# Interleaving the token-mean products of a Fourier mix with its first output tile, and taking two half tiles before the rest

## The reference, cut to what matters

```
def fourier_mix(a, w_out):
    B, L, D = a.shape
    ag = a.reshape(B, L, FNET_GROUPS, FNET_GROUP_DIM).astype(jnp.float32)
    f = jnp.fft.fft2(ag, axes=(1, 3), norm="ortho").real
    return f.astype(a.dtype).reshape(B, L, D) @ w_out

def first_block(x, c, ...):
    sh1, sc1, gt1, sh2, sc2, gt2 = ada_params(c, w_mod[i], b_mod[i])
    a_lat = modulate(h_lat, g_norm_mix[i], sh1, sc1)
    y_lat = fourier_mix(a_lat, w_fnet_out[j])
    h_lat = h_lat + gt1 * y_lat
    h_lat = h_lat + gt2 * conv_ffn(modulate(h_lat, g_norm_ffn[i], sh2, sc2), ...)
```

## Time and profile before

| what | value |
|---|---|
| median of 3 runs | 1563.52 us (1563.16 to 1564.2) |
| the profiled execution, own time | 1563.37 us |
| its span | 1561.6 us |
| TensorE busy | 1544.6 us, 99% |
| GpSimd busy | 999.9 us, 64% |
| VectorE busy | 748.0 us, 48% |
| ScalarE busy | 310.2 us, 20% |
| share of the chain that ended last | TensorE 96% |

### The profile page before, as it was taken

How to read it: one execution, slowest core, us unless ns; L and a number is a source line. 1 busy time by engine, 2 the same in 40 slices (tenths; PEclk the granted TensorE clock), 3 DMA queues, 4 the chain that set the end, 5 groups by cost and what they waited for, 6 DMA issues and landing times.

```text
span 1561.6 us, 19509 instructions
## 1 busy us (share of the span) xinstructions
PE 1544.6 (99%) x7096; PEld 1287.6 (82%) x7096; DVE 748.0 (48%) x876; ACT 310.2 (20%) x478; POOL 999.9 (64%) x792
## 2 busy tenths in 40 slices
PE   7999999999999999999999999999999999999998
PEld 6998888888887888888888888888888888888887
DVE  7875455560427565244154665456576434443013
ACT  6542111110111001112032122212322111111001
POOL 4736666666666666766555576475567667676664
PEclk9999999999999999999999999999999999999999
DMA  9962333333332333332323232232233333333231
GB/s 371 404 241 81 94 103 98 94 95 94 99 112 86 96 101 100 106 95 81 107 68 95 72 96 86 80 94 81 67 94 95 94 99 100 97 94 94 95 102 61
DMA packets 218119, 172.52 MB, mean 110 GB/s; under 512 B 5216, under 2 KB 191968, under 8 KB 218080
## 3 DMA queue, kind: packets, MB, share of 16 engines
q1 hardware_dynamic: 218080, 171.98, 35.2%
HBM read 169.86 MB, written 2.10 MB: 110 GB/s over the span
## 4 chain that ended last, share of the span: by engine, by line
PE 96%; DVE 1%; DMA 1%; SPq 1%; issue 0%; ACT 0%; DVEq 0%
PE ps L572 32%; PE ps L575 32%; PE ps L576 32%; DMA mod_early<-in_w_mod_t 1%; DVE act_lo L1402 0%; SPq L314 0%; SPq L322 0%; PE ps L655 0%; PE ps L905 0%; DVE gates L1750 0%; DVE mod_early L1313 0%; PE ps L759 0%; DVE res L1522 0%; SPq L334 0%; PE ps L688 0%
## 5 line engine op out<-in xcount | busy, mean ns | idle before, releaser
L550 POOL TENSOR_TENSOR w_lo<-raw,w_hi 128x1024 fp32r<-128x1024 f32 x248 | 623.0, 2512 | 20.7
L572 PE MATMUL ps<-act_hi,w_hi 128*128 128x512 f32 (+1 forms) x1304 | 506.1, 388 | 0.2 <-DVE act_lo L1402 0.2
L576 PE MATMUL ps<-act_lo,w_hi 128*128 128x512 f32 (+1 forms) x1304 | 503.0, 386 | 0.0
L575 PE MATMUL ps<-act_hi,w_lo 128*128 128x512 f32 (+1 forms) x1304 | 503.0, 386 | 0.0
L547 POOL TENSOR_TENSOR w_hi<-raw,zero 128x1 fp32r<-128x1 f32 x248 | 56.2, 226 | 488.5 <-PE ps L572 488.5
L572 PEld LDWEIGHTS ps<-act_hi,w_hi 128*128 128x128 f32 x1304 | 245.7, 188 | 51.5 <-issue 1.7
L575 PEld LDWEIGHTS ps<-act_hi,w_lo 128*128 128x128 f32 x1304 | 245.7, 188 | 49.7 <-issue 1.4
L576 PEld LDWEIGHTS ps<-act_lo,w_hi 128*128 128x128 f32 x1304 | 245.7, 188 | 49.2
L548 POOL TENSOR_SCALAR w_hi<-raw 128x1023 fp32r<-128x1023 f32 x248 | 266.5, 1075 | 0.0
L572 PE MATMUL ps<-wide_hi,w_hi 128*128 128x512 f32 (+2 forms) x624 | 239.9, 384 | 0.4 <-DVE wide_lo L1281 0.4
L576 PE MATMUL ps<-wide_lo,w_hi 128*128 128x512 f32 (+2 forms) x624 | 239.4, 384 | 0.0
(11 more groups left out here) (193 smaller groups left out, 1440.2 us busy)
## 6 DMA issues: line engine op xcount, KB each, us to landing
raw<-in_w_in SPq DMA_DIRECT2D x88, 512.0 KB, 4.0
gates<-in_w_mod_t SPq DMA_DIRECT2D x20, 1024.0 KB, 11.3
raw<-in_w_ffn_up SPq DMA_DIRECT2D x40, 512.0 KB, 3.9
raw<-in_w_ffn_down SPq DMA_DIRECT2D x22, 512.0 KB, 3.7
raw<-in_w_ff_gate SPq DMA_DIRECT2D x22, 512.0 KB, 3.9
raw<-in_w_ff_up SPq DMA_DIRECT2D x22, 512.0 KB, 3.9
raw<-in_w_ff_down SPq DMA_DIRECT2D x22, 512.0 KB, 3.8
raw<-in_w_r_out SPq DMA_DIRECT2D x16, 512.0 KB, 3.5
```

The source lines that it names most:

```text
L550: nc.gpsimd.tensor_tensor(w_lo[:, two, :], raw[:, slot, :], f32(w_hi[:, two, :]), SUB).then_inc(split_done, 1)
L572: ins = mm(o, w, a, start=start, stop=False)
L575: mm(o, wl, a, start=False, stop=False)
L576: return mm(o, w, al, start=False, stop=stop)
```

## The change

Four things change, and no product is added or left out.

1. On TensorE the 16 token-mean products no longer stand in one block. Two of them follow each of the eight products of the second half of mix tile 0. The wait ahead of them is for one Fourier tile more (`3 * (KT - 1)`), because `dc_psum` moves from bank 3 to bank 5.
2. The second half of mix tile 1 comes next, ahead of the wait for column 0. Tile 1 is thus taken in two halves of 256 tokens, where it was one piece of 512.
3. Panel 1 is split earlier: `fnet_hi(1)` on ScalarE ahead of the loop over the Fourier tiles, `fnet_lo(1)` on GpSimd ahead of the eight low parts `act_lo`.
4. SyncE's and VectorE's code stays as it is.

```diff
+DC_BANK = 5
...
-        dc_psum = ps[:, 3, 0:KT]
+        dc_psum = ps[:, DC_BANK, 0:KT]
...
             fnet_lo(0)
+            fnet_lo(1)
...
-            for m in range(1, 6):
+            for m in range(2, 6):
                 fnet_lo(m)
...
-            pe.wait_ge(f_made, 3 * (KT - 2))
-            pe.wait_ge(dc_step, DC_SUMMED)
-            for m in range(KT):
+            def dc_products(m):
+
                 g, e = m // 2, m % 2
                 for k in range(2):
                     c0 = k * 2 * GROUP + e * P
                     ins = mm(dc_psum[:, m:m + 1], raw[:, 2, c0:c0 + P], udc[:, 2 * g + k:2 * g + k + 1], start=k == 0, stop=k == 1)
-            ins.then_inc(dc_step, 1)
+                return ins
...
+            pe.wait_ge(f_made, 3 * (KT - 1))
+            pe.wait_ge(dc_step, DC_SUMMED)
+            t_ = halves[1]
+            pe.wait_ge(fnet_split, 1)
+            for b in range(KT):
+                pe.wait_ge(f_ready, b + 1)
+                product(ps[:, FNET_BANKS[0], t_], *w_block(fnet_weights(0), b), act_hi[:, b, t_], act_lo[:, b, t_], b == 0, b == KT - 1)
+                ins = dc_products(b)
+            ins.then_inc(dc_step, 1)
+            pe.wait_ge(fnet_split, 2)
+            tile(ps[:, FNET_BANKS[1], t_], None, fnet_weights(1), act_hi[:, :, t_], act_lo[:, :, t_])
+            pe.wait_ge(dc_step, DC_READY)
+
             for n, (m, t_) in enumerate(FNET_TILES):
...
-                if n == 0:
-                    t_ = halves[1]
-                    tile(ps[:, FNET_BANKS[n], t_], None, fnet_weights(m), act_hi[:, :, t_], act_lo[:, :, t_], (f_ready, 0))
-                    pe.wait_ge(dc_step, DC_READY)
+                if n < 2:
                     t_ = halves[0]
...
             shift_sum(2)
+            fnet_hi(1)
...
             f_hi(KT - 1)
-            fnet_hi(1)
             act.wait_ge(dc_step, DC_DONE)
```

## The result

| | before | changed |
|---|---|---|
| median | 1563.99 us (1563.16 to 1565.1, 14 runs) | 1567.39 us (1566.72 to 1568.91, 14 runs) |
| ratio | | 1.0022, 95% interval 1.0015 to 1.0029 |
| profiled execution, span | 1561.6 us | 1565.5 us |

The change costs 3.4 us, more than the 3.1 us (0.2%) that I had called the bound of what can be told, though the interval reaches down to 0.15%. The forecast was 1564.2, the range ended at 1565.7.

A forecast was written before the change was run, and what follows sets the result against it. TensorE has 96% of the chain, but the DMA queue sets the time at `half_sums(0)`, swallowing TensorE's 1.11 us gain. 1563.37 + 0.7 of hole = 1564.1, stated as 1564.2 for the median; 8-in-10 range 1562.9 to 1565.7.

The forecast's parts named there:

- TensorE's own sum: TensorE from token-mean products to start of tile 2: 16.30 us before, 15.19 after, a gain of 1.11 us.
- Panel 1's split: Earlier split on ScalarE and GpSimd fits their idle gaps; first low part 0.5 us late, cost 0 on the path.
- DC_DONE 3.0 us later: Signal that the last token-mean product is done, awaited by ScalarE, VectorE and SyncE: at 55.12 instead of 52.10.
- VectorE's cover: VectorE's existing 3.2 us of DMA waits between 60 and 75 us absorb its 3.0 us delay at column 0.
- A hole of 0.7 us: DMA engines idle 0.7 us before panel 3, issued at 55.3; all later landings and the squares slip by 0.7.
- The clock: Rival, 12%: TensorE's idling at `half_sums(0)` drops its clock, costing 0.7 + 1.6 us; 1565.8.
- a wait of 2.0 us: TensorE reaches `half_sums(0)` at 91.95 and waits for squares ready at 94.0, where it waited 0.25 us.
- The rival on the other side: Slower, 8%: clock falls early in the interleaved stretch, panel 3 is issued later, hole of 2.2 to 2.7 us; 1566.0.
- The "Nothing" rival: Rival, 20%: transfers in flight at 55.3 hide panel 3's start, TensorE's gain still lost at `half_sums(0)`; 1563.5, +-0.2.
- The rival of a gain: Rival, 12%: squares tied to TensorE's own pieces, not a DMA landing, so `half_sums` comes earlier; -1.1 us, 1562.4.

The follow-up runs named there:

- e6: Changed kernel with the token-mean products in one block again, ahead of the second half of tile 0; 1565.32 us, ratio 1.0008 to before.
- e9: Changed kernel, SyncE issuing part 4's first chunk ahead of the wait for the token-mean products, panels 3 and 5 in old order; 1563.69 us.
- e2: Changed kernel, VectorE working on two more tiles of part 2 before it waits for column 0; 1567.07 us, ratio 1.0022 to before.
- e7: Kernel before, SyncE's issue of panel 3 held until panel 2's low part is done, 4.9 us later; 1568.78 us, ratio 1.0031.
- e3: Kernel before, SyncE's issue of panel 3 held until panel 1's low part is done, 2.5 us later; 1565.20 us, ratio 1.0009.
- e10: e9 with first-half sums moved behind the fourth product of piece 10 and second-half sums one step later; 1562.94 us, ratio 0.9993 to before.
- e11: e10 run once more, nothing further changed; 1562.90 us, ratio 0.9994 to the kernel before.
- e1: Changed kernel, SyncE issuing panel 5 and part 4's first chunk ahead of panel 3; 1567.30 us, ratio 1.0014 to before.
- e4: Changed kernel with 24 surplus products of 256 columns on TensorE ahead of `half_sums(0)`, result unread; 1565.69 us, ratio 1.0013 to before.

## Why the prediction was wrong

- **TensorE's own sum: right in kind, a little large.** Tile 2 starts at 64.30, 64.05 without this execution's 0.25; forecast 63.9. The gain is 0.86 us instead of 1.11. The clock held in this stretch, as said. Most of the missing 0.25 is a later start, 49.14 where 48.75 and the offset give 49.00, and the eight interleaved groups, 6.45 us (49.14 to 55.59) instead of 6.37.
- **Panel 1's split: right.** The next copy on ScalarE came at 39.97, and TensorE saw no new wait. e6 and e9 have it and lose no 3 us by it.
- **DC_DONE 3.0 us later: nearly right.** Column 0 on ScalarE is at 55.76, forecast 55.3, and 0.25 of the difference is this execution's: 3.2 us later.
- **VectorE's cover: right.** It was held 3.1 us and then waited for the DMA again: its tile of 72.23 stands at 74.65, released by a landing. e2 takes away 2.4 us of the hold, and the squares stay late.
- **"A hole of 0.7 us": the step that failed.** It measured 1.9 us in the share of the DMA engines and 2.1 in the squares. The landing of panel 3 itself was what I said: issued at 55.8, landed 3.3 us later, 0.97 later than before and 0.72 without the offset. But I took the lateness of this one landing for the idle time of the engines, and as the sum's only term it put the squares at +0.7.

Three things were missing in that step. Quarter microseconds of the changed kernel show the first two:

```profile
54.00:54.25 0.25, 0.25 (x4) 0.25 (x4) 0.00 (x0) 0.00 (x0) 0.00 (x0) 1.00 1.11 426
54.25:54.50 0.25, 0.25 (x5) 0.25 (x4) 0.00 (x0) 0.00 (x0) 0.00 (x0) 1.00 0.77 287
...
54.75:55.00 0.25, 0.25 (x4) 0.25 (x4) 0.00 (x0) 0.00 (x0) 0.00 (x0) 1.00 0.48 189
...
55.50:55.75 0.25, 0.25 (x4) 0.25 (x4) 0.00 (x0) 0.00 (x0) 0.00 (x0) 1.00 0.25 98
...
56.25:56.50 0.25, 0.25 (x4) 0.25 (x3) 0.25 (x1) 0.25 (x1) 0.00 (x0) 1.00 0.00 0
56.50:56.75 0.25, 0.25 (x5) 0.25 (x4) 0.25 (x1) 0.25 (x1) 0.00 (x0) 1.00 0.00 0
...
57.50:57.75 0.25, 0.25 (x5) 0.25 (x4) 0.25 (x1) 0.00 (x0) 0.25 (x1) 1.00 1.00 410
```

First, the 16 DMA engines run dry one after the other. The trace records 16 steps of the semaphore for each transfer, and the landing is the last of them. Panel 4's came from 54.74 to 56.85, so most engines had nothing to do long before the landing (issued at 39.35, 17.5 us to landing). Second, panel 3, issued at 55.80, has its first packet at 56.77, 0.97 us later (0.96 in e7), and the share is back at 1.00 from 57.50. The delay at the other end is shorter: panel 4's last packet ended at 56.36, 0.49 us before its landing. Third, the landing of panel 3 hid the hole. In the kernel before its 16 steps were spread from 55.59 to 58.13, in the changed kernel from 58.64 to 59.11: on average they came 2.3 us later, the last only 0.98. Behind the hole all engines started together, so the slowest one had caught up with the others.

The landings behind it were 1.1 us late (without the offset of 0.25) up to the second chunk, and 2.1 from panel 6 on. At the second of these steps the profile shows one packet of another DMA queue, which starts at 66.06 and takes 0.96 us. From the DMA view of 66 to 68 us (queue and kind, packets, MB, share of 16 engines):

```profile
q8 instruction: 1, 0.02, 3.0%
```

Panel 6's last step came 1.08 us behind the last but one, where the chunk ahead of it had 0.15, and the distance stayed. The same shows in e3 and e7 behind their packet at 70.9 and 70.7; in the kernel before, with its steps still spread over some 2.4 us, the packet at 70.7 moved the last step hardly at all. That this packet is what put one engine back is inferred from time and size, not tested. By this reading the squares would have been only some 1.1 us late without it (an estimate), and that 1.9 us of idle share went with 2.1 us of late squares is in part chance.

How far the queue covers a late issue can be read off the profiled executions. Panel 3's issue was at 55.09 in e3, 55.46 in e2, 55.80 in the changed kernel and 57.38 in e7, and the squares were 1.69, 1.96, 2.37 and 3.90 us late. Each issue less its lateness gives 53.4 to 53.5; in e9 the chunk's issue, at 53.12, was ahead of that, and there was no hole. It fits the share, which falls from 54.25 on, less the 0.97 us from issue to first packet. The kernel before issued at 52.3 and had 1.1 us to spare; the change moved the issue by 3.5.

The Trainium skill (DMA: Bandwidth & Descriptors, "Anatomy of one DMA") says that most of a DMA's fixed cost of some 2.0 us lies behind the last byte, in the confirmation of the write; it says so of DMAs that GpSimd issues, and here SyncE issues them. The trace doesn't agree with this split: 0.97 us lie ahead of the first packet and 0.49 behind the last. Its sum of an estimated 3.2 us for the landing, used in the prediction, was near the measured 3.3.

- **The clock: a rival at 12%, and it came.** I priced it rightly (1.6; measured 1.5) and its sum, 1565.8, lacked only the larger hole: 1565.8 + 1.4 = 1567.2. It was probably the failed step that brought it on: I forecast a wait of 2.0 us, and it was 3.04; no run had one of 2.0. Waits of 1.0 (e9) and 1.6 us (e3) left the clock alone in the profiled executions, 3.04, 3.6 and 3.9 lost it, and one of 3.0 (e2) kept it.
- **The rival on the other side** had the wrong place (the clock inside the interleaved stretch). Its remark that the hole decides, and not VectorE, held.

The "Nothing" rival falls with e3: what is in flight hides only the first 1.1 us of a later issue. The rival of a gain falls too, but e10 and e11 show what it would have needed.

Open: the single runs of the kernel before lie in two groups, around 1563.2 and around 1564.8. A clock that falls behind the block of token-mean products in some executions and not in others would do it, but no profile without that fall was taken.

## What to carry to other kernels

Where an order is changed on one engine, look for the DMA issue that waits for the moved work: in a stretch where the DMA engines are full, the time to protect is when the first engines run dry, which the DMA share shows and a landing doesn't (here the share fell from 54.25 on and the landing came at 56.85). The issue has to come about another microsecond ahead of that (0.97 us from issue to first packet here). Each microsecond by which it missed that time was a microsecond for what hangs on later landings (e3, e7). Put a transfer that is free to go ahead of the one that waits, but no more than fills the hole, since what waits behind may itself release a later issue (e1). A gain on the bounding engine counts only up to its next wait in program order; move the wait into the work (e10). An idle stretch can cost the clock on top: here those of 3.04, 3.6 and 3.9 us did, those of 1.0 and 1.6 us and one of 3.0 us didn't.

## What the runs showed of the hardware

- Surplus matmuls in an idle stretch made the program 1.4 to 1.7 us faster (e4); the granted clock behind it stayed at 1.00 instead of 0.50.
- Single-column float32 products, 32 instructions in a row, were shown as 3.50 of 3.50 us busy and were followed by half the clock. With three 256-column products between every four of them the clock held at 1.00 in the executions that I profiled.
- A 512 KB DMA issued into a nearly empty queue landed after 3.3 us; in the full queue of the kernel before it took 5.8.
- The 16 steps of one transfer's semaphore came 2.1 us apart from first to last (changed kernel, panel 4), and 0.5 us apart behind a stretch in which all engines had been idle (panel 3).
- From an issue on SyncE to its first packet with all DMA engines idle it took 0.97 us (changed kernel) and 0.96 us (e7), from the last packet to the landing 0.49 and 0.47 us.
